# The chunked recurrence of an RWKV mixer: its matrix products, copies and adds put in another order, and one accumulated term folded into an add

## What is computed

```python
def wkv_scan(s0, r, w, k, v, a, b, reverse):
    def step(s, inp):
        r_t, w_t, k_t, v_t, a_t, b_t = inp
        sa = jnp.einsum('bhvk,bhk->bhv', s, a_t)
        s = s * w_t[:, :, None, :] + sa[..., :, None] * b_t[:, :, None, :] + v_t[..., :, None] * k_t[:, :, None, :]
        return s, jnp.einsum('bhvk,bhk->bhv', s, r_t)
```

## Time and profile before

| | us |
|---|---|
| median of 3 runs | 3041.14 (3032.96 to 3041.2) |
| the profiled execution | 3047.39 |
| its span, first to last instruction | 3045.5 |
| PE busy | 2514.2 (83%) |
| PEld busy | 1934.9 (64%) |
| DVE busy | 1639.6 (54%) |
| ACT busy | 987.2 (32%) |
| POOL busy | 631.3 (21%) |
| mean granted TensorE clock | 0.886 |

### The profile page before, as it was taken

One profiled execution on the slowest core, in us unless ns is written; L12 is line 12 of the kernel. 1 busy time (PEld: TensorE's weight loads), 2 busy tenths in 40 slices (PEclk: granted clock), 3 DMA queues, 4 the chain that ended last, 5 costly groups with the idle time before them and its releaser, 6 DMA issues. The chain is left out here.

```text
span 3045.5 us, 57305 instructions
## 1 busy us (share of the span) xinstructions
PE 2514.2 (83%) x23846; PEld 1934.9 (64%) x23846; DVE 1639.6 (54%) x2057; ACT 987.2 (32%) x1546; POOL 631.3 (21%) x618
## 2 busy tenths in 40 slices
PE   4698997869989379997857888888763799999993
PEld 1586654546757368886336667774553788888882
DVE  2793447521114322565545556552336499999993
ACT  2111442210013320001324333332211087777772
POOL 0221357212210023220045444430000010110000
PEclk8899999989999679998569999995875599999996
DMA  9232004321113211110231011101533099999993
GB/s 381 70 135 79 10 1 133 100 96 52 34 56 124 94 49 63 49 42 18 102 93 31 18 25 30 26 4 56 190 119 138 20 391 403 398 388 398 399 380 132
DMA packets 132726, 405.60 MB, mean 133 GB/s; under 512 B 55090, under 2 KB 64946, under 8 KB 102690
## 3 DMA queue, kind: packets, MB, share of 16 engines
q1 hardware_dynamic: 119268, 359.53, 31.6%
q0 software_dynamic: 4608, 16.78, 2.3%
q10 hardware_dynamic: 8640, 26.19, 2.2%
HBM read 346.85 MB, written 55.61 MB: 132 GB/s over the span
## 5 line engine op out<-in xcount | busy, mean ns | idle before, releaser
L3039 DVE TENSOR_TENSOR ex_wl<-ew_raw,ex_wh 128x2048 fp32r<-128x2048 f32 x192 | 435.8, 2290 | 42.6 <-ACT ex_wh L3001 39.0
L3001 ACT ACTIVATE ex_wh<-ew_raw 128x2048 fp32r<-128x2048 f32 x192 | 367.6, 1919 | 216.8 <-PEq L89 109.3
L125 PE MATMUL sp_acc<-b2h_hi,sp_wh 128*128 128x512 f32 (+1 forms) x528 | 194.8, 369 | 11.7 <-POOL sp_wl L1614 11.7
L125 PE MATMUL sp_acc<-b2h_lo,sp_wh 128*128 128x512 f32 (+1 forms) x528 | 194.5, 368 | 0.0
L125 PE MATMUL sp_acc<-b2h_hi,sp_wl 128*128 128x512 f32 (+1 forms) x528 | 194.3, 368 | 0.0
L2162 ACT ACTIVATE rc_xt<-rc_ps 128x256 f32<-128x256 f32 x200 | 67.7, 389 | 197.2 <-PE rc_ps L2331 196.6
L2922 POOL DMA_INDIRECT x<-ex_o,ex_at x16 | 26.5, 1656 | 493.1 <-DVE ex_o L3062 493.1
L1100 DVE TENSOR_TENSOR merge_sg<-b_pj,merge_sg 128x512 f32<-128x512 f32 x16 | 11.1, 693 | 218.0 <-ACT merge_sg L1086 218.0
L2229 DVE TENSOR_TENSOR rc_x<-rc_x,rc_ps 128x256 f32<-128x256 f32 x160 | 60.2, 418 | 120.4 <-PE rc_ps L2317 120.1
L125 PE MATMUL merge_acc<-merge_hh,merge_wh 128*128 128x512 f32 x256 | 101.5, 396 | 26.4 <-POOL merge_wl L119 21.1
L125 PEld LDWEIGHTS sp_acc<-b2h_hi,sp_wh 128*128 128x128 f32 x528 | 100.1, 190 | 28.7 <-POOL sp_wl L1614 12.1
(11 more groups left out here) (465 smaller groups left out, 6364.6 us busy)
## 6 DMA issues: line engine op xcount, KB each, us to landing
ew_raw<-in_exp_gate SPq DMA_DIRECT2D x64, 1024.0 KB, 7.5
ew_raw<-in_exp_up SPq DMA_DIRECT2D x64, 1024.0 KB, 9.7
ew_raw<-in_exp_down SPq DMA_DIRECT2D x64, 1024.0 KB, 8.2
b_pj<-in_ada_w SPq DMA_DIRECT2D x24, 1024.0 KB, 19.1
rc_ac<-ac SPq DMA_DIRECT2D x40, 256.0 KB, 3.8
merge_w<-in_w_merge SPq DMA_DIRECT2D x16, 512.0 KB
ac<-rp_ac SPq DMA_DIRECT2D x4, 2048.0 KB, 7.2
pr_w<-in_w_main SPq DMA_DIRECT2D x14, 512.0 KB
```

What stands on the lines that cost most here:

```text
L125: ins = nc.tensor.matmul(out, w[a][:, k, :], h[b][:, k, cols], start=(first and n == 0), stop=(last and n == 2))
L3001: nc.scalar.activation(wh[:, n % RING], raw[:, n % RING], ACT.Copy).then_inc(q["w_hi"], 1)
L3039: V.tensor_tensor(wl[:, n % RING], raw[:, n % RING], wh[:, n % RING].bitcast(f32), ALU.subtract).then_inc(q["w_lo"], 1)
```

## The change

On PE, `gs` goes: `solved` has one term. The keys are issued in two halves, the first ahead of `advanced` of level 0, the second behind it, and `right_side_of_state` moves behind them. `outputs` moves from level 2 ahead to just behind `advanced` of level 1, and the transposes of bst and kst from there to behind `products` of level 2. On ACT, g is copied as soon as `right_side` is done (`g_crossed`), gs isn't copied, and the copies of the b and k rows move behind the transpose copy of level 2. `right_side_of_state` on PE now waits for the copies of g. On DVE a new `right_side` adds the state's half out of PSUM to g between levels 0 and 1, the two lk products are moved apart (one behind `masked` of level 1, one behind `advanced` of level 1), and the four adds to y are issued crossed, crossed, stayed, stayed.

```diff
@@ scalar @@
-                def right_side(count):
-                    for d in range(2):
-                        b, s = t[d], q[d]
-                        act.wait_ge(joint["g_done"], count)
-                        hold(act, passed)
-                        A.activation(paired(b["g"][:]), crossed(2, d), ACT.Copy).then_inc(s["g_ready"], 1)
-                        A.activation(b["gs"][:], stayed(2, d, 1), ACT.Copy).then_inc(s["g_ready"], 1)
-
...
                     transposed(i, 0, sl)
                     if old is not None:
-                        right_side(i)
+                        copy("g_crossed", i, lambda b: paired(b["g"][:]), lambda d: crossed(2, d), "g_copied")
                     transposed(i, 1, sl)
                     if old is not None:
                         copy("u_done", i, lambda b: paired(b["u"][:]), lambda d: crossed(2, d), "u_ready", -1.0)
+                    transposed(i, 2, sl)
                     for d in range(2):
...
-                    transposed(i, 2, sl)
                     if following is not None:
                         filled(i + 1, 1 - sl)
@@ vector @@
                 def outputs(c):
+                    dve.wait_ge(joint["y_done"], c - CTX_CK + 1)
+                    for n in range(2):
+                        for d in range(2):
+                            yv = y[:, :, ds(y_at(c, d), CK)]
+
+                            for o in range(2) if n == 0 else (d,):
+                                dve.wait_ge(q[o]["y_added"], 2 * (c - CTX_CK) + 1 + n)
+                            hold(dve, passed)
+                            if n == 0:
+                                V.tensor_tensor(paired(yv), crossed(2, d), paired(yv), ALU.add).then_inc(q[d]["y_added"], 1)
+                            else:
+                                V.tensor_tensor(yv, stayed(2, d, 1), yv, ALU.add).then_inc(q[d]["y_added"], 1)
+
+                def right_side(count):
                     for d in range(2):
                         b, s = t[d], q[d]
...
+                        dve.wait_ge(joint["g_done"], count)
+                        V.tensor_tensor(b["g"][:], stayed(2, d, 1), b["g"][:], ALU.add).then_inc(s["g_ready"], 1)
...
                 def body(i, sl, half, old, here, following):
                     masked(i, 0)
                     advanced(i, 0, sl)
-                    for d in range(2):
-                        b, s = t[d], q[d]
-                        dve.wait_ge(joint["pk_done"], i + 1)
-                        V.tensor_tensor(paired(b["lk"][:, sl]), crossed(3, d, 2 * CK), over(T.plus[d][:]), ALU.mult).then_inc(s["lk_ready"], 1)
+                    if old is not None:
+                        right_side(i)
                     masked(i, 1)
+                    factor(i, sl, 0)
                     advanced(i, 1, sl)
+                    factor(i, sl, 1)
                     masked(i, 2)
@@ tensor @@
                 def right_side_of_state(count, sl):
                     for d in range(2):
                         pe.wait_ge(q[d]["state"], count)
-                    pe.wait_ge(g_crossed, count)
+                    for d in range(2):
+                        pe.wait_ge(q[d]["g_copied"], count)
                     staying(2, 1, lambda b: b["ar"][:, sl, :, 0:CK], lambda b: b["S"]).then_inc(joint["g_done"], 1)
+
+                def keys(sl, j):
+                    return crossing(3, 2 * CK, (lambda b: b["kst"][:, sl], lambda b: b["ar"][:, sl]), pairs=(j,))
 
                 def solved(count, sl):
                     for d in range(2):
-                        pe.wait_ge(q[d]["g_ready"], 2 * count)
+                        pe.wait_ge(q[d]["g_ready"], count)
                         pe.wait_ge(q[d]["inverse"], count)
-                    crossing(2, CK, (lambda b: b["xt"][:, sl], lambda b: b["g"]), (lambda b: b["xt"][:, sl], lambda b: b["gs"])).then_inc(joint["u_done"], 1)
+                    crossing(2, CK, (lambda b: b["xt"][:, sl], lambda b: b["g"])).then_inc(joint["u_done"], 1)
...
                     x_turned(i, 0, sl)
                     if old is not None:
                         right_side(i, 1 - sl)
-                        right_side_of_state(i, 1 - sl)
-                    advanced(i, 0, sl)
                     for d in range(2):
                         pe.wait_ge(q[d]["stk"], i + 1)
-                    crossing(3, 2 * CK, (lambda b: b["kst"][:, sl], lambda b: b["ar"][:, sl])).then_inc(joint["pk_done"], 1)
+                    keys(sl, 0)
+                    advanced(i, 0, sl)
+                    keys(sl, 1).then_inc(joint["pk_done"], 1)
+                    if old is not None:
+                        right_side_of_state(i, 1 - sl)
                     x_turned(i, 1, sl)
                     products(i, 1, sl)
                     if old is not None:
                         solved(i, 1 - sl)
                     advanced(i, 1, sl)
+                    if old == "all":
+                        outputs(i, 1 - sl)
+                    x_turned(i, 2, sl)
+                    products(i, 2, sl)
                     for d in range(2):
                         pe.wait_ge(q[d]["lk_ready"], i + 1)
                     for d in range(2):
...
                         last.then_inc(s["rows_done"], 1)
-                    x_turned(i, 2, sl)
-                    products(i, 2, sl)
-                    if old == "all":
-                        outputs(i, 1 - sl)
                     advanced(i, 2, sl)
```

More of the change, by code:

```diff
@@ L1983, in rwkv_chunks @@
                  "lk_ready", "b_rows", "k_rows", "v_rows", "t1_ready", "xt_done", "xt_next", "x_next", "inverse",
-                 "g_ready", "u_ready", "y_added", "summed", "state", "own")
+                 "g_copied", "g_ready", "u_ready", "y_added", "summed", "state", "own")
         ka_loaded, ka_made, cleared, passed = ph.sem("ka_loaded"), ph.sem("ka_made"), ph.sem("cleared"), ph.sem("passed")
-        joint = {n: ph.sem(n) for n in ("pm_done", "pl_done", "pk_done", "t1_done", "xp_done", "g_done", "u_done", "y_done", "s_done", "xi_done")}
-        g_crossed, y_crossed = ph.sem("g_crossed"), ph.sem("y_crossed")
+        joint = {n: ph.sem(n) for n in ("pm_done", "pl_done", "pk_done", "t1_done", "xp_done", "g_done", "g_crossed", "u_done", "y_done", "s_done", "xi_done")}
+        y_crossed = ph.sem("y_crossed")
         ps = [ph.ps(f"ps{n}", [P, 2, 512]) for n in range(4)]
@@ L1997, in rwkv_chunks @@
                 b[n] = ph.sb(f"{n}{d}", [P, 2, HP, CK])
-            for n in ("e_neg", "tmp", "t1", "vst", "v", "g", "gs", "u", "sum", "S"):
+            for n in ("e_neg", "tmp", "t1", "vst", "v", "g", "u", "sum", "S"):
                 b[n] = ph.sb(f"{n}{d}", [P, HP, CK])
@@ L2211, in _ @@
                 chunks(act, body)
-                right_side(NCK)
+                copy("g_crossed", NCK, lambda b: paired(b["g"][:]), lambda d: crossed(2, d), "g_copied")
                 copy("u_done", NCK, lambda b: paired(b["u"][:]), lambda d: crossed(2, d), "u_ready", -1.0)
@@ L2269, in advance_state, with factor @@
                         V.tensor_tensor(b["S"][:], b["sum"][:], b["e_end"][:, sl].to_broadcast([P, HP, CK]), ALU.mult).then_inc(s["state"], 1)
+                def factor(c, sl, d):
+                    b, s = t[d], q[d]
+                    dve.wait_ge(joint["pk_done"], c + 1)
+                    V.tensor_tensor(paired(b["lk"][:, sl]), crossed(3, d, 2 * CK), over(T.plus[d][:]), ALU.mult).then_inc(s["lk_ready"], 1)
                 def body(i, sl, half, old, here, following):
@@ L2303, in _ @@
                 chunks(dve, body)
+                right_side(NCK)
                 outputs(NCK - 1)
@@ L2308, in _, with crossing @@
                 M = nc.tensor.matmul
-                def crossing(n, w, *terms):
-                    for j, s in product(range(HP // 2), range(2)):
+                def crossing(n, w, *terms, pairs=range(HP // 2)):
+                    for j, s in product(pairs, range(2)):
                         for i, (l, r) in enumerate(terms):
@@ L2377, in right_side @@
                         pe.wait_ge(q[d]["v_rows"], count)
-                    crossing(2, CK, (lambda b: b["lk"][:, sl, :, 0:CK], lambda b: b["v"])).then_inc(g_crossed, 1)
+                    crossing(2, CK, (lambda b: b["lk"][:, sl, :, 0:CK], lambda b: b["v"])).then_inc(joint["g_crossed"], 1)
                 def right_side_of_state(count, sl):
```

## The result

| | before | after |
|---|---|---|
| median, us | 3038.91 (4 runs, 3032.96 to 3041.2) | 3008.04 (4 runs, 3003.66 to 3009.39) |
| ratio | 1 | 0.9899, 95% interval 0.988 to 0.9918 |
| profiled execution, us | 3047.39 | 3009.39 |
| its span, us | 3045.5 | 3007.6 |

The changed kernel is faster by 31 us, 1.0%. The forecast was 22 us less against the median, so the direction and the range held and the size was nearly a third too small.

A forecast was written before the change was run, and what follows sets the result against it. The prediction took the recurrence as bound in turn by the chain through the levels and PE's instruction arrival. Terms -20, +2 and -3, rounded up for the tail, gave -22 us: 3019 us against the median, range 2997 to 3040.

The forecast's parts named there:

- Two bounds in turn: Recurrence stage: bound in turn by the chain through the levels and the rate at which PE's instructions arrive.
- `solved`: -20 us: PE, each chunk: 64 fewer instructions save 1.06 us of fetch time a chunk, 20 us over 19 chunks.
- The lower view: `solved` on PE: its second term costs only about 0.2 us a chunk on the chain, 4 us in all.
- g: free: DVE between levels 0 and 1: two adds of 0.75 us hide in 1.3 us of PE work; uncovered, 14 us.
- lk moved, 0: DVE, level 1: each lk product hides behind `masked` or `advanced`, where DVE waits for PE; no gain or loss.
- Keys split, 0: PE around `advanced` of level 0: split keys and moved state's right side sum the same; 0, within ±0.3 us a chunk.
- `outputs` against the transposes, +2 us: PE, levels 1 and 2: exchange of near-equal times, with a wait for u of 0.1 us in 16 chunks.
- Adds to y, -3: DVE ahead of the level-3 mask: alternated adds take 1.6 instead of 2.0 us; half counted over 16 chunks.
- 1 for the tail: Short tail: loses one `solved` term and changes two copies for two adds; rounded up by 1 us.
- Rival 1: The chain gives more: 2.2 us a chunk, 41 us in all, so 3000 us; chance 0.17.
- Rival 2: Instruction stream is not the limit, or the gain is taken back: only -5 us, 3036 us; chance 0.17.
- Rival 3: Slower: PE stands at `outputs` for u because g's add makes `solved` 0.75 us late; 3056 us, chance 0.10.

The follow-up runs named there:

- the dose: Changed kernel plus one unread block of 32 loads and 32 products a chunk in level 4; median 3030.4 us, distance 460.0, 20.4 us more than the changed kernel.
- the shortened chain: Changed kernel without PE's repeated waits, same products and order; median that of the changed kernel, first-to-last distance of the inverse's end 4 us shorter.
- e10_lk: Changed kernel with both lk products back ahead of the mask of level 1; 13 us slower by medians, 7.6 by distance.
- e12_narrow: Changed kernel with 64 columns instead of 128 in `lower` and the keys, same instruction count; 4 us less by medians, 2 by distance.
- fold alone: Kernel before with g copied, the state's half added on DVE and one term in `solved`, old order kept; 13 us less than before.
- e9_swap: Changed kernel with lk, `outputs`, the transposes and ACT's row copies back in their old places; median 3031.0 us, 20 to 23 us slower.
- e11_shift: Changed kernel with 128 unread instructions once, ahead of the first chunk; 6.5 us slower by median, 7 by distance.
- e2_order: Changed kernel with gs still copied by ACT and a second term in `solved`; 8.5 us less than the kernel before.

## Why the prediction was right, and what was off

**Two bounds in turn.** Shown for the two parts of the stage. In the later 15 chunks the dose cost 21 us, and the shortened chain and the narrower products gained next to nothing; in the first four the dose cost nothing and the shortened chain gained 5 to 9 us (a shift alone gave 3.7 there). That the stage takes the longer of the two also within a chunk, fetch by fetch, so that a delay of the chain (the late mask of e10_lk) is paid where no fetch is late, fits all runs but is argued.

**`solved`: -20 us.** Within the new order 20 us by distance, 21 to 24 by medians, and the dose gives 20 back. The lower view (4 us) is refuted and the taken one held in its sum, but by luck: 1.06 us in each of 19 chunks isn't what happened. The first four chunks, which have no outputs and so fewer instructions, gained nothing, and in the later 15 the term was worth 1.5 us each and the dose 1.4. The 4.24 us that priced a fetch are a mean spacing with waits of the chain in it. Why 64 instructions cost more than their share of it where PE's queue is dense is open; their 0.56 us of PE's own time are a candidate, against which e12_narrow speaks.

**g: free.** Right in the changed kernel, but not for the reason that I gave alone. I priced the uncovered add at 14 us and lk's move at 0, as independent steps. They aren't: add and lk together (2.0 us) don't fit ahead of the mask. Without lk's split the fold loses 8 to 13 us, which is enough to explain why fold (13) and order (8.5) together gave 31 and not 21. **That is one step that failed: lk moved, 0.** It was free of cost and also the cover of another step. (The transposes that moved with it aren't readers of lk, as I wrote; they wait for it because they write into ps3, which it is read from.)

**Keys split, 0.** Not run by itself. The fold alone and e9_swap differ by this split, the place of the state's right side with its wait, and the adds to y; in total they are alike (3028.1 and 3031.0, 451.5 and 454.8), but not by parts: with the split the first four chunks took 95.0 us against 89.2, the later 15 took 359.8 against 362.3. My bound of ±0.3 us a chunk is passed in the first four; whether by the split or by place alone no run tells. So 0 isn't shown.

**`outputs` against the transposes, +2 us.** This step failed: about 7.5 us were gained. By parts that is 8 us in the later 15 chunks and none in the first four, which have no outputs. The wait for u that I priced was 0.5 us, once in 230 us. What made the exchange pay is not settled. Equal time on PE isn't equal instruction count (128 instructions in 1.1 us against 16 in 1.0), so it changes how dense the queue is around the fetches; no run isolates that, and e11_shift shows that 7 us, 10.7 in the later 15 chunks, can come from place alone.

**Adds to y, -3.** The mask starts 0.56 us sooner instead of 0.4; what that is worth stays open: 0.5 us by distance, 8 to 10 by medians.

**Sum.** About -22 for the fold within the new order and -8.5 for the order alone make the measured -31; this holds by the way the two are taken, and each has its share of place in it. I had -20 and -1, with 1 for the tail. Rival 1 had a surplus in the right direction, but its 41 us were not reached, and that the adds brought it isn't shown. Rival 2 is refuted by the dose and by e2_order. Rival 3 needed `solved` to wait for DVE; the profile has no such wait.

Of the rule that crossing a 16 KiB boundary of the instruction stream is mostly hidden (the Trainium skill, Runtime: NRT & Kernel Launch, Instruction fetch mechanics): the packets have that size, but here 68 breaks of 65 us in all end, but for one, at the same distance behind a packet, and 64 instructions a chunk cost 20 us. The measurement decides: with some 255 instructions used up in 4 us it is not hidden.

## What to carry to other kernels

Where an unrolled program issues many short matrix products, count its instructions and the instruction packets: a run of like products that breaks off for half a microsecond or more with no releaser, time and again at the same distance behind a packet, is most likely waiting for its own program. Then a removed instruction can be worth more than its own time (64 of them 1.5 us a chunk here) and a removed wait nothing. But test both in each part of the stage: in the first four chunks, with fewer instructions, it was the other way round. And take a difference of a few microseconds between two orders for nothing until a mere shift of the program has been measured. And when work is moved onto another engine, add up everything that then stands ahead of the next link of the chain on that engine's queue: two moves that are free each (0.75 and 1.3 us on DVE) made the mask 0.6 us late together.

## What the runs showed of the hardware

A semaphore increment of its own on PE's queue cost 0.11 to 0.13 us (144 and 161 us for 1280), as much as six or seven weight loads of a dense run (32 in 0.56 us). And the granted clock of the first 27 us of the stage was anything from 0.56 to 0.90 over the 14 profiles, in kernels with the same program ahead of it; the first inverse ended at 1593.7 us with 0.63 there and at 1587.6 with 0.90. That the low clock is the cause was not tried.
